# RWKV head norm computed token by token, half of it inside the second chunk's solve, with w_out issued right behind the solve

## The reference, cut to what matters

```python
y = _rwkv7_scan(rh, heads(decay), kh, vh, -kk, kk * ah)          # b, T, 8 heads, 64
mean = jnp.mean(y, axis=-1, keepdims=True)
var = jnp.mean(jnp.square(y - mean), axis=-1, keepdims=True)
y = ((y - mean) * lax.rsqrt(var + RWKV_GN_EPS)).reshape(b, T, RWKV_D) * f32(ln_w) + f32(ln_b)
bonus = jnp.sum(rh * kh * f32(r_k), axis=-1, keepdims=True) * vh
return (y + bonus.reshape(b, T, RWKV_D)) * g
...
mix = jnp.concatenate([y_ssd, y_rwkv], axis=-1).astype(h.dtype) @ w_out[l]
```

## Time and profile before

| | |
|---|---|
| median of 3 runs | 825.14 us (821.84 to 825.64) |
| the profiled execution | 824.1 us, its span 822.3 us |
| mean granted TensorE clock | 0.983 of full |
| busy: PE, DVE, ACT, POOL | 787.0, 548.8, 393.5, 71.4 us |

### The profile page before, as it was taken

One profiled execution on the slowest core, in us unless ns is written; L12 is line 12 of the kernel. 1 busy time (PEld: TensorE's weight loads), 2 busy tenths in 40 slices (PEclk: granted clock), 3 DMA queues, 4 the chain that ended last, 5 costly groups with the idle time before them and its releaser, 6 DMA issues.

```text
span 822.3 us, 17167 instructions
## 1 busy us (share of the span) xinstructions
PE 787.0 (96%) x7490; PEld 663.3 (81%) x7490; DVE 548.8 (67%) x866; ACT 393.5 (48%) x623; POOL 71.4 (9%) x98
## 2 busy tenths in 40 slices
PE   7999978989899999999999999999999999999996
PEld 6788866768686888888886877588878888888885
DVE  4678856646486899999676787654476476664443
ACT  5458441110415566677564764152554375553333
POOL 1142011202001110111001100000200200000000
PEclk9999997989999999999999999999999999999999
DMA  9971230203028365545774264112647145555001
GB/s 333 393 267 66 103 116 3 105 2 106 2 102 290 121 201 186 189 183 183 282 296 173 104 243 167 47 56 103 264 146 265 44 161 196 198 222 222 29 1 52
DMA packets 66555, 127.93 MB, mean 156 GB/s; under 512 B 3760, under 2 KB 27568, under 8 KB 66352
## 3 DMA queue, kind: packets, MB, share of 16 engines
q1 hardware_dynamic: 65168, 122.92, 41.4%
q0 software_dynamic: 592, 2.69, 0.9%
q10 hardware_dynamic: 720, 1.23, 0.4%
HBM read 125.78 MB, written 1.05 MB: 154 GB/s over the span
## 4 chain that ended last, share of the span: by engine, by line
PE 70%; DVE 16%; ACT 5%; issue 4%; DMA 2%; SPq 1%; POOL 1%; DVEq 0%; POOLq 0%
PE bank L502 21%; PE bank L610 19%; DVE arena L490 8%; PE bank L607 7%; DVE arena L1975 3%; PE bank L2062 3%; DMA ring<-in_w_in_dram 2%; PE bank L1246 2%; ACT arena L481 2%; PE bank L756 2%; PE bank L731 2%; PE bank L1265 1%; PE bank L2256 1%; SPq L447 1%; PE bank L2524 1%
## 5 line engine op out<-in xcount | busy, mean ns | idle before, releaser
L490 DVE SCALAR_TENSOR_TENSOR arena<-ring,arena 128x1024 f16<-128x1024 f32 x194 | 230.1, 1232 | 79.4 <-ACT arena L481 79.0
L502 PE MATMUL bank<-hg,arena 128*128 128x256 f16 x2496 | 275.9, 273 | 0.9 <-DVE arena L490 0.8
L502 PEld LDWEIGHTS bank<-hg,arena 128*128 128x128 f16 x2496 | 242.9, 98 | 33.4 <-issue 3.5
L481 ACT ACTIVATE arena<-ring 128x1024 f16<-128x1024 f32 x194 | 191.9, 1045 | 89.4 <-PE bank L610 51.7
L610 PE MATMUL bank<-arena 128*128 128x256 f16 x1296 | 142.2, 273 | 0.2 <-DVE arena L490 0.2
L610 PEld LDWEIGHTS bank<-arena 128*128 128x128 f16 x1296 | 126.6, 98 | 15.5 <-issue 0.9
L607 PE MATMUL bank<-mix,ring 128*128 128x256 f32 x256 | 55.7, 379 | 1.1 <-ACT arena L1907 1.1
L607 PEld LDWEIGHTS bank<-mix,ring 128*128 128x128 f32 x256 | 48.5, 190 | 8.4 <-issue 1.9
L517 ACT ACTIVATE hg<-h,params 128x256 f16<-128x256 f32 (+1 forms) x40 | 20.0, 499 | 57.3 <-DVE h L2470 43.6
L1975 DVE SCALAR_TENSOR_TENSOR arena<-arena,params 128x256 f32<-128x256 f32 x88 | 36.6, 477 | 0.7 <-ACT arena L2009 0.7
L502 PE MATMUL bank<-xv,arena 128*128 128x256 f16 x288 | 32.1, 273 | 0.0
(11 more groups left out here) (368 smaller groups left out, 965.3 us busy)
## 6 DMA issues: line engine op xcount, KB each, us to landing
ring<-in_w_in_dram SPq DMA_DIRECT2D x12, 2048.0 KB, 9.2
ring<-in_ffn_w_up_dram SPq DMA_DIRECT2D x22, 1024.0 KB, 7.5
ring<-in_w_ff_dram SPq DMA_DIRECT2D x8, 2048.0 KB, 8.8
ring<-in_w_ff_dram SPq DMA_DIRECT2D x16, 1024.0 KB, 6.1
ring<-in_ffn_w_down_dram SPq DMA_DIRECT2D x11, 1024.0 KB, 5.9
ring<-in_w_out_dram SPq DMA_DIRECT2D x8, 1024.0 KB, 6.5
ring<-in_w_xk_dram SPq DMA_DIRECT2D x2, 2048.0 KB, 10.2
ring<-in_w_xv_dram SPq DMA_DIRECT2D x2, 2048.0 KB, 7.9
```

Of the source, the lines that this page charges most:

```text
L481: nc.scalar.activation(quarter(halves_of(chunk)[0], chunk, q), quarter(slot(*chunk), chunk, q), ACT.Copy, scale=W_SCALE).then_inc(*mark("w ...
L490: nc.vector.scalar_tensor_tensor(quarter(halves_of(chunk)[1], chunk, q), quarter(slot(*chunk), chunk, q), W_SCALE, quarter(halves_of(chunk ...
L502: mm = nc.tensor.matmul(out_, weight[a][:, k, cols], src[:, k, b, :], start=(first and i == 0), stop=(last and i == 2), skip_group_check=True)
```

## The change

- The mean and the variance are no longer sums by matmul in channel-major layout. A chunk's `y` is turned by four PE transposes (`pe_y_turn`) so that tokens lie on partitions; DVE sums over each head's 64 columns (`TENSOR_REDUCE`, 128x512 to 128x8) and centres; ACT squares; DVE sums; ACT takes the root and DVE the reciprocal of 128x8; one multiplication follows (`y_unit`), and four transposes bring it back (`pe_y_back`).
- For chunk 0 this runs inside chunk 1's solve: the turns are `fill(1)` and `fill(9)`, the DVE steps stand behind levels 0, 1 and 2, and POOL does the multiplication, between its copies for chunk 0 and for chunk 1.
- The bonus: ACT instead of DVE scales the products, the two sums are `fill(3)` and `fill(5)` of chunk 0, POOL multiplies by `V_`, and ACT adds `ln_b` to it. The gate's matmuls are `fill(7)` and `fill(9)` of chunk 0. Both go to banks 2 and 5 and are copied to SBUF by ACT.
- `pe_rwkv_end` is gone. w_out waits for `U`, `RB` and the keys of chunk 1 instead, and follows the solve at once. Chunk 1's turns stand inside it: the first behind its 4th product, the one back behind its 16th.
- POOL finishes `mix` for the first 128 tokens, DVE for the last 128.

```diff
-        def narrow(pe, name, ktiles, src, src_ready, label, free, order=None):
+        def narrow(pe, name, ktiles, src, src_ready, label, free, order=None, between=None):
...
                         for m in range(KT):
                             last_row = product(i, kk, m)
+                            if i == order[0] and (kk, m) in between:
+                                between[kk, m]()
...
             def fill(n):
                 if n % 2 == 0:
                     pe_mem_part(pe, 8 * c + n // 2)
+                elif c == 0 and n in (3, 5):
+                    pe_bonus_sums(pe, n // 2 - 1)
+                elif c == 0 and n in (7, 9):
+                    pe_gate(pe, n // 2 - 3)
+                elif c and n == 1:
+                    pe_y_turn(pe, 0)
+                elif c and n == 9:
+                    pe_y_back(pe, 0)
                 elif n < 10:
                     pe_keep_clock(2)
...
                 pe.wait_ge(*at("XT diagonal", c, g))
+                pe.wait_ge(*(at("y scaled", 3) if c else at("gate out", g)))
...
+                if c and n == 0:
+                    dve_y_centre(dve, 0)
                 if n in (1, 3):
                     mem_low(dve, 4 * c + n // 2 + 2)
+                if c and n == 1:
+                    dve_y_variance(dve, 0)
+                if c and n == 2:
+                    dve_y_rate(dve, 0)
...
         def act_rwkv_chunk(act, c):
-            for n in range(4 * c + 2, 4 * c + 5):
-                mem_high(act, n)
+            if c == 0:
+                act_bonus(act)
+                mem_high(act, 2)
+                for i in range(2):
+                    act_bonus_out(act, i)
+                mem_high(act, 3)
+                for i in range(2):
+                    act_gate_out(act, i)
+                mem_high(act, 4)
+            else:
+                act_bonus_shift(act)
+                mem_high(act, 6)
+                act_y_squares(act, 0)
+                act_y_root(act, 0)
+                mem_high(act, 7)
+                act_y_scaled(act)
...
+        def dve_y_centre(dve, c):
+            bank = heads(banks[TOKEN_BANK[c]][:, :])
+            dve.wait_ge(*at("y turned", c))
+            nc.vector.tensor_reduce(ysum[c], bank, AX.X, ALU.add).then_inc(*mark("rwkv_end_vector"))
+            dve.wait_ge(*so_far("rwkv_end_vector"))
+            if c:
+                dve.wait_ge(*at("y back", 0))
+            nc.vector.scalar_tensor_tensor(heads(YC), along(ysum[c], RW_HD), -1.0 / RW_HD, bank, ALU.mult,
+                                           ALU.add).then_inc(*mark("rwkv_end_vector", "y centred", c))
...
+        def y_unit(eng, ops, name, c):
+            eng.wait_ge(*at("y rate", c))
+            ops.tensor_tensor(heads(YC), heads(YC), along(yrate[c], RW_HD), ALU.mult).then_inc(
+                *mark(name, "y unit", c))
...
         def dve_rwkv_end(dve):
+            dve_y_centre(dve, 1)
+            dve_y_variance(dve, 1)
+            dve_y_rate(dve, 1)
+            y_unit(dve, nc.vector, "rwkv_end_vector", 1)
+            dve.wait_ge(*at("y back", 1))
+            dve.wait_ge(*at("bonus shifted", 3))
+            for j in range(4):
+                nc.vector.scalar_tensor_tensor(Y[:, j, C:2 * C], quarters(BACK_BANK[1])[:, j, :],
+                                               par("rwkv_ln_w", j), BONUS[:, j, C:2 * C], ALU.mult,
+                                               ALU.add).then_inc(*mark("rwkv_end_vector"))
...
-            pe_rwkv_end(pe)
             narrow(pe, "w_out", KT, mix, lambda k: ("mix1", k), "out1",
-                   lambda b: ("variance root", 1) if b > 1 else ("centred", b))
+                   lambda b: (("U", 1, 1), ("RB", 1, 1), ("keys", 2), ("keys", 3))[b],
+                   between={(0, 3): lambda: pe_y_turn(pe, 1), (1, KT - 1): lambda: pe_y_back(pe, 1)})
...
             for c in range(NC_):
                 dve_rwkv_chunk(dve, c)
-                if c == 0:
-                    dve_bonus(dve)
```

More of the change, by code:

```diff
@@ L1825, in pool_rwkv_chunk, with heads, pe_bonus_sums, pe_gate @@
                         *mark("solve_pool", *(("XT diagonal", c, g) if b == 3 else ())))
-        def pe_rwkv_end(pe):
+        def heads(v):
+            return v.rearrange("p (n d) -> p n d", d=RW_HD)
+        def pe_bonus_sums(pe, i):
+            pe.wait_ge(*at("bonus products"))
+            nc.tensor.matmul(banks[2 + 3 * i][:, :], head_ones, flat(A_)[:, 512 * i:512 * i + 512], start=True,
+                             stop=True).then_inc(*mark("rwkv_end_pe", "bonus bank", i))
+        def pe_gate(pe, i):
@@ L1829, in pe_rwkv_end, with pe_y_turn @@
             pe.wait_ge(*at("lora gate"))
             pe.wait_ge(*at("gate weights"))
+            pe.wait_ge(*at("bonus copied", i))
+            for j in (2 * i, 2 * i + 1):
+                mm = nc.tensor.matmul(halves(2 + 3 * i)[:, j % 2, :], gate_w[:, j * P:(j + 1) * P], GLO,
+                                      start=True, stop=True)
+            mm.then_inc(*mark("rwkv_end_pe", "gate bank", i))
+        TOKEN_BANK, BACK_BANK = (5, 1), (5, 2)
+        def pe_y_turn(pe, c):
             for g in range(2):
-                pe.wait_ge(*at("y out", 1, g))
@@ L1833, in pe_rwkv_end @@
-                pe.wait_ge(*at("RB", 1, g))
-            pe.wait_ge(*at("keys", 3))
+                pe.wait_ge(*at("y out", c, g))
             for j in range(4):
[L1836 to L1852, removed]
+                mm = nc.tensor.transpose(quarters(TOKEN_BANK[c])[:, j, :], Y[:, j, c * C:(c + 1) * C], ident)
@@ new lines, in act_bonus, with act_bonus_out, act_gate_out @@
+                nc.scalar.activation(A_[:, j, :], A_[:, j, :], ACT.Copy, scale=par("rwkv_r_k", j)).then_inc(
+                    *mark("rwkv_end_act", *(("bonus products",) if j == 3 else ())))
+        def act_bonus_out(act, i):
+            act.wait_ge(*at("bonus bank", i))
+            nc.scalar.activation(flat(BONUS)[:, 512 * i:512 * i + 512], banks[2 + 3 * i][:, :], ACT.Copy).then_inc(
+                *mark("rwkv_end_act", "bonus copied", i))
+        def act_gate_out(act, i):
+            act.wait_ge(*at("gate bank", i))
+            nc.scalar.activation(flat(GATE)[:, 512 * i:512 * i + 512], banks[2 + 3 * i][:, :], ACT.Copy).then_inc(
+                *mark("rwkv_end_act", "gate out", i))
@@ new lines, in pool_bonus_values, with act_bonus_shift @@
+        def pool_bonus_values(pool):
+            for i in range(2):
+                pool.wait_ge(*at("bonus copied", i))
+            nc.gpsimd.tensor_tensor(flat(BONUS), flat(BONUS), flat(V_), ALU.mult).then_inc(
+                *mark("rwkv_end_pool", "bonus"))
+        def act_bonus_shift(act):
+            act.wait_ge(*at("bonus"))
+            for j in range(4):
+                nc.scalar.activation(BONUS[:, j, :], BONUS[:, j, :], ACT.Identity,
+                                     bias=par("rwkv_ln_b", j)).then_inc(*mark("rwkv_end_act", "bonus shifted", j))
@@ new lines, in dve_y_rate, with act_y_scaled @@
+        def dve_y_rate(dve, c):
+            dve.wait_ge(*at("y root", c))
+            nc.vector.reciprocal(yrate[c], yrate[c]).then_inc(*mark("rwkv_end_vector", "y rate", c))
+        def y_unit(eng, ops, name, c):
+            eng.wait_ge(*at("y rate", c))
+            ops.tensor_tensor(heads(YC), heads(YC), along(yrate[c], RW_HD), ALU.mult).then_inc(
+                *mark(name, "y unit", c))
+        def act_y_scaled(act):
+            act.wait_ge(*at("y back", 0))
+            for j in range(4):
+                nc.scalar.activation(Y[:, j, 0:C], quarters(BACK_BANK[0])[:, j, :], ACT.Copy,
+                                     scale=par("rwkv_ln_w", j)).then_inc(*mark("rwkv_end_act", "y scaled", j))
@@ new lines, in pool_y_end @@
+        def pool_y_end(pool):
+            pool.wait_ge(*at("y scaled", 3))
+            pool.wait_ge(*at("bonus shifted", 3))
+            pool.wait_ge(*at("gate out", 1))
+            nc.gpsimd.tensor_tensor(Y[:, :, 0:C], Y[:, :, 0:C], BONUS[:, :, 0:C], ALU.add).then_inc(
+                *mark("rwkv_end_pool"))
+            pool.wait_ge(*so_far("rwkv_end_pool"))
+            pool.wait_ge(*at("mem quarter used", MEM_QUARTERS - 1))
+            nc.gpsimd.tensor_tensor(mix[:, 4:8, 0:C], Y[:, :, 0:C], GATE[:, :, 0:C], ALU.mult).then_inc(
+                *mark("rwkv_end_pool", "mix1 first tokens"))
```

86 lines of the change are left out of this document (42 added, 44 removed).

## The result

| | before | changed |
|---|---|---|
| median of 4 runs each | 824.3 us (821.84 to 825.64) | 814.99 us (813.77 to 818.56) |
| the profiled execution, its span | 824.1, 822.3 | 818.56, 816.7 |

The ratio of changed to before is 0.9894, 95% interval 0.9859 to 0.993; run once more beside other kernels it was 0.9898 (0.988 to 0.9916). So the change makes the kernel about 8.7 us (1.06%) faster, by the interval 5.8 to 11.6 us. The forecast was 815.5.

A forecast was written before the change was run, and what follows sets the result against it. PE was taken as the bound, busy 787.0 of 822.3 us, so time comes from its standstills and its work. The terms summed to -9.7 us, 814.4 from the profiled 824.1, forecast as 815.5 against the runs' median; range 812.5 to 820.5.

The forecast's parts named there:

- (a): End of chunk 1's solve: w_out follows the `y` products at once, starting at 212.2 instead of 222.15, -9.95 us.
- (b): Inside w_out: eight fp32 transposes for chunk 1's turns add 1.0 us (bounds 0.9 and 1.3).
- (c): Inside w_out: 5.2 us of products cover chunk 1's norm chain of 4.0 to 5.2, wait 0 (upper bound 1.5).
- (d): Chunk 0's fills: bonus sums and gate matmuls outlast the constant matmuls, +1.6 us (bounds 0.9 and 2.3).
- (e): Start of chunk 1: bonus scaling leaves DVE's queue, so PE's wait of 1.40 falls to about 0.35, -1.05 us.
- (f): Chunk 0's norm on DVE, inside chunk 1's solve: centring +0.2 us, second reduce ahead of level 2's mask +0.7.
- (g): Start of chunk 1: the clock's fall to the lower level is likelier gone than not, -2.2 us.
- The comparison by busy share: Chunk 1's start: about 2.0 of 3.4 us busy should keep the clock, as 1.80 did at 211.3.
- Rival 1: The clock falls again at chunk 1's start, so the gain is 7.7 us, time 817.4; chance 0.37.
- Rival 2: More PE waits, for POOL's multiplication or the turn back in w_out: 2 to 4 us, 818 to 821; chance 0.11.

The follow-up runs named there:

- e1: Changed kernel with both of chunk 1's turns put ahead of w_out again instead of inside it: 821.19 us, ratio 0.9974.
- e8: Kernel before, with one and four constant matmuls in front of the two waits for X of chunk 1's level 0: 824.64 us, ratio 1.0015.
- e4: Changed kernel with four DVE multiplications of 128x256 by one put back at the start of chunk 1: 815.29 us, ratio 0.9908.
- e9: The changed kernel run again without edits, as yardstick for the last group of runs: 814.92 us, ratio 0.9898.
- e2: Changed kernel with one and four constant matmuls in front of the two waits for X of chunk 1's level 0: 814.29 us, ratio 0.9893.
- e10: Changed kernel with bonus and gate matmuls cut into 256-column pieces, one for each odd fill of both chunks: 814.55 us, ratio 0.989.
- e6: Changed kernel with the remaining constant matmuls left out: 814.35 us, ratio 0.9881.
- e5: Changed kernel with every remaining pair of constant matmuls replaced by four fp32 transposes on the same bank: 815.47 us, ratio 0.9897.
- e3: Changed kernel with the second reduce of chunk 0's norm moved behind level 2's update: 815.0 us, ratio 0.9903.

## Why the prediction held, term by term

Measured in us, each from the stage table unless said:

- **(a)** -9.95: measured **-9.87** (12.79 to 2.92). **(b)** +1.0: **+0.92**. **(c)** 0: **0**; the chain is 4.1 us in the forecast 4.0 to 5.2, and e1 shows what stands on it: 7.2 us later, and 1.9 of low clock, which no term or rival had.
- **(d)** +1.6: PE's own work grew by **+1.9**: chunk 0 without gaps and without a fall is 38.5 and 38.6 for before and e8, and 40.2 to 40.6 for the changed kernel's code (e1 to e4, e9). In e9 "dX" of levels 1 and 2 follow "P" by 1.71 us instead of 1.19, so a long fill costs 0.52 and not 0.43 to 0.47; only the last, `fill(9)`, comes cheaper, at 0.25 (3.73 us from memory part to memory part instead of 3.48). The bound of 2.3 held. But the sum took PE's time for the kernel's, and in these runs gaps and falls in chunk 0 differ by more than that between executions.
- **(e)** -1.05: **-1.06** on the wait itself (1.40 to 0.34); e4 gives 0.65 to 0.8 of it back.
- **(f)** +0.9: **0 to +0.2**. This step failed. Level 2's "mask" row had seemed to begin when `mem_low` ended; it began 0.52 us behind the start of PE's "P" as at every level, and `mem_low` ended at that time by chance. And "dX" did not hang on it: the mask starts at 186.84 in the kernel before, "dX" at 187.51, 0.67 behind, while in the changed kernel the mask starts at 189.16 and "dX" at 189.43, 0.27 behind. So some 0.4 us of the reduce were hidden under PE's own fill. In e2 "dX" of levels 1 and 2 follow "P" by 1.20 and 1.19 us, as before; in the changed kernel level 2's follows by 1.37 (188.06 to 189.43).
- **(g)** -2.2, the fall gone: wrong as a step. It came in eight of the nine profiles of kernels with this start on PE (not in e10's); only its length was halved, from 6.8 to about 3.4 us. Priced in chunk 1 without gaps: 2.3 with and without it before (37.9, 35.6), 1.4 with the change (35.9, 34.4 to 34.6). So **-0.9**. The comparison by busy share failed: 2.05 us of 3.4 here, with a fall; 1.80 of 3.4 at 211.3, without. What differs in the rows is what PE did: here two groups of 32x32 tiles and a group of transposes, there fp32 work on 64 to 128 rows. That this is the reason was not tried, and it can't be all of it, since e10 has the same rows and the same 2.04 of 3.4 us (177.0 to 180.4) without a fall.

The sum of what was measured is -9.87 + 0.92 + 1.9 - 1.06 + 0.1 - 0.9 = -8.9, against -8.7 from the ratio. The forecast had -9.7, 0.8 too much: (f) was put 0.8 too dear, the gain of (g) 1.3 too high and (d) 0.3 too cheap. That the median still came within 0.5 us of 815.5 is luck, since the forecast started from 825.14, 0.8 us above the median that before had in the sample of four (824.3), and the two errors cancel. The larger samples beside the experiments, 11 to 17 runs, put before at 822.9 to 823.6. Rival 1 is the nearer to what the profiles show, at 1.3 us in place of its 2.0. Rival 2's waits did not come: PE waits for POOL nowhere, for ACT only at chunk 1's start as before (1.49 us), and for the turn back not at all.

## What to carry to other kernels

A serial chain between two long matmul phases is paid in full while PE waits for it; making it shorter, with the sums moved away, brought 2.1 us here, and covering it the other 6 to 7 (e1). So put the first products of the next phase, which don't need its result, between its steps. Where PE stands still with no releaser named, for 0 to 2.2 us a chunk and differently from execution to execution, the median of five runs can't price 1 or 2 us of work on it: read the stage without its gaps and falls. And read the granted clock of every stage, also of those that the change doesn't touch, and profile twice, before you explain one or two us.

## What the runs showed that I had not expected

PE's gaps without a releaser stand at fixed places of its instruction stream. In e8 they are ahead of the last 50 matmuls of level 1's "dX", ahead of level 2's "dX", and ahead of the last 12 of level 3's "P". From the first to the second are 50 + 12 + 64 + 2 = 128 matmuls, from the second to the third 64 + 12 + 52 = 128, each with its weight load: 256 instructions. The changed kernel's:

```profile
150.44 0.30 PE L1573 MATMUL bank<-arena 32*32 32x16 f32 x12 [1.30 <-issue]
...
190.43 0.25 PE L1584 MATMUL bank<-arena 32*32 32x16 f32 x7 [0.34 <-issue]
...
194.43 0.37 PE L1584 MATMUL bank<-arena 32*32 32x16 f32 x21 [0.67 <-issue]
```

e2 has five matmuls more ahead of chunk 1's levels, and its gaps are five matmuls earlier (12 left of 64 in place of 7); e6 has two fewer in chunk 0 and its gap is two later (10 left). By level 3 of chunk 1, e5 has eight more (29 left in place of 21) and e6 eight fewer (13 left). The rows of e2 and e6:

```profile
182.93 1.27 PE L1252 MATMUL bank<-xk,mix 128*128 128x256 f16 x10 [0.27 <-issue]
...
186.65 0.30 PE L1586 MATMUL bank<-arena 32*32 32x16 f32 x12 [0.71 <-issue]
```

```profile
150.60 0.29 PE L1571 MATMUL bank<-arena 32*32 32x16 f32 x10 [1.30 <-issue]
```

Their length changes from execution to execution (0.17 to 1.30 us at one place with the same code). It doesn't follow from how early PE gets there: in the changed kernel's code it reaches the place in level 3's "P" 16.9 to 17.3 us behind the chunk's start, and both the longest gap and the shortest stand at 17.3. The Trainium skill, "Runtime: NRT & Kernel Launch", Instruction fetch mechanics, says that an engine's instructions come in blocks of 256, and that the cost of a block's boundary is mostly hidden. The spacing agrees with it. If the gaps are such boundaries, the second half doesn't hold here, where a level of some 140 matmuls passes in 3.3 us and one gap costs up to 1.3 (1.50 once, in e3). That the gaps are fetches is argued from the spacing and from how it moves with the matmuls put in and taken out; what sets their length stays open.

A second fall of the clock, in chunk 0 at 151 to 152, is in four of the fourteen profiles, each behind a gap of 1.03 to 1.30 us; with gaps under 1 us there was none, and three with 1.01 to 1.30 us had none. It costs 1.3 us (43.38 - 1.50 against 41.15 - 0.60). With the gap it makes up most of what sets the profiled execution of the changed kernel, 818.56, above its median. In chunk 1 it is alike: e3's second fall follows a gap of 1.50 us and e6's two gaps over 1 us, while e8 has one of 1.16 us and no fall. So long gaps and these falls go together, and no run tried whether the one makes the other.
